# The search scores of the sample rows summed over heads in two passes of a split source, with the first projection tile of u placed among the last prompt scores

## What is computed

```python
def indexer_select(qi, wi, ki_all, q_pos, topk):
    s = jnp.einsum('bqhd,bld->bqhl', qi, ki_all) * (IDX_DIM ** -0.5)
    score = jnp.einsum('bqhl,bqh->bql', jax.nn.relu(s), wi) * (IDX_HEADS ** -0.5)
    score = jnp.where(admissible, score, NEG_INF)
    _, idx = lax.top_k(score, topk)
```

## Time and profile before

| | us |
|---|---|
| median of 3 runs | 1353.95 (1350.81 to 1354.22) |
| the profiled execution | 1354.13 |
| its span from first to last instruction | 1352.3 |
| PE busy | 1309.8 |
| DVE busy | 696.0 |
| POOL busy | 584.0 |
| ACT busy | 534.1 |

### The profile page before, as it was taken

How to read it: one execution, slowest core, us unless ns; L and a number is a source line. 1 busy time by engine, 2 the same in 40 slices (tenths; PEclk the granted TensorE clock), 3 DMA queues, 4 the chain that set the end, 5 groups by cost and what they waited for, 6 DMA issues and landing times.

```text
span 1352.3 us, 25244 instructions
## 1 busy us (share of the span) xinstructions
PE 1309.8 (97%) x9720; PEld 1212.9 (90%) x9720; DVE 696.0 (51%) x1611; ACT 534.1 (39%) x1075; POOL 584.0 (43%) x607
## 2 busy tenths in 40 slices
PE   5989999999999999999999999999999999999998
PEld 4957999995666899878999999999999999999997
DVE  5368997777985222227934434434544333333445
ACT  5345787747776322325533334334300110111034
POOL 5432975441331311321277667667433333333610
PEclk9999999999999999999999999999999999999999
DMA  6340113310001775782233323323531332133203
GB/s 195 74 104 17 46 42 112 94 50 1 1 12 37 265 231 192 237 281 95 80 112 126 111 81 127 111 80 127 192 112 47 111 112 93 66 112 111 63 1 128
DMA packets 143550, 141.68 MB, mean 105 GB/s; under 512 B 21081, under 2 KB 111321, under 8 KB 143424
## 3 DMA queue, kind: packets, MB, share of 16 engines
q1 hardware_dynamic: 124933, 116.31, 27.0%
q10 hardware_dynamic: 17842, 21.94, 4.5%
q0 software_dynamic: 656, 1.84, 0.6%
HBM read 111.87 MB, written 26.50 MB: 102 GB/s over the span
## 4 chain that ended last, share of the span: by engine, by line
PE 81%; DVE 6%; ACT 2%; issue 1%; POOL 0%; ACTq 0%; DVEq 0%; POOLq 0%
PE bank L2096 74%; PE bank L2272 2%; PE bank L2338 2%; DVE junk L1669 1%; ACT sjunk L1119 1%; PE bank L2417 1%; DVE prob L1762 1%; PE bank L2141 1%; DVE lack L1673 1%; PE bank L2605 0%; DVE hid_lo L2021 0%; DVE sqacc L1884 0%; DVE hn_lo L1897 0%; PE bank L2298 0%; DVE cum L1728 0%
## 5 line engine op out<-in xcount | busy, mean ns | idle before, releaser
L2096 PE MATMUL bank<-hid_hi,w_hi 128*128 128x384 f32 (+1 forms) x672 | 217.6, 324 | 0.0
L2096 PE MATMUL bank<-hid_lo,w_hi 128*128 128x384 f32 (+1 forms) x672 | 216.0, 324 | 0.8 <-DVE hid_lo L2021 0.8
L2096 PE MATMUL bank<-hid_hi,w_lo 128*128 128x384 f32 (+1 forms) x672 | 216.2, 322 | 0.0
L2053 DVE TENSOR_TENSOR acc<-bank,acc 128x384 f32<-128x384 f32 x168 | 87.6, 523 | 199.3 <-PE bank L2096 199.3
L690 POOL TENSOR_TENSOR w_hi<-w_raw,zero 128x256 fp32r<-128x256 f32 x108 | 68.7, 636 | 206.1 <-PE bank L2096 190.7
L2096 PE MATMUL bank<-xn_hi,w_hi 128*128 128x384 f32 (+1 forms) x456 | 151.3, 332 | 2.5 <-POOL w_lo L692 1.7
L904 POOL TENSOR_TENSOR w_hi<-w_raw,zero 128x1024 fp32r<-128x1024 f32 x29 | 54.9, 1894 | 221.3 <-PE bank L2096 203.3
L2096 PE MATMUL bank<-xn_lo,w_hi 128*128 128x384 f32 (+1 forms) x456 | 148.1, 325 | 0.0
L2096 PE MATMUL bank<-xn_hi,w_lo 128*128 128x384 f32 (+1 forms) x456 | 147.5, 323 | 0.0
L1416 ACT ACTIVATE hid_hi<-hraw 128x1056 fp32r<-128x1056 f32 x32 | 32.7, 1078 | 257.1 <-DMA hraw<-hidden_dram 130.2
L2096 PE MATMUL bank<-hi_T,hn_hi 128*128 128x264 f32 x448 | 127.5, 285 | 0.0
(11 more groups left out here) (300 smaller groups left out, 3212.0 us busy)
## 6 DMA issues: line engine op xcount, KB each, us to landing
w_raw<-in_w_ff_dram SPq DMA_DIRECT2D x50, 512.0 KB, 3.5
hraw<-hidden_dram SPq DMA_DIRECT2D x16, 1056.0 KB, 7.3
page<-in_cache_k_dram SPq DMA_DIRECT2D x64, 256.0 KB, 3.5
page<-in_cache_v_dram SPq DMA_DIRECT2D x64, 256.0 KB, 3.6
hidden_dram<-stg ACTq DMA_DIRECT2D x56, 264.0 KB, 2.0
w_raw<-in_w_in_dram SPq DMA_DIRECT2D x18, 512.0 KB, 3.7
wr<-in_w_ff_dram SPq DMA_DIRECT2D x14, 512.0 KB, 4.5
xrow<-in_x_prompt_dram SPq DMA_DIRECT2D x8, 512.0 KB, 8.2
```

The source lines that it names most:

```text
L2053: nc.vector.tensor_tensor(v, ps[:, 0:w], v, ALU.add).then_inc(freeof(("dn", gi, m, g)), 1)
L2096: return nc.tensor.matmul(out, lhsT, rhs, start=start, stop=stop)
```

## The change

The sum over heads is made from a split source. `hsum` is copied to `hsum_r` (rounded type, on ACT), `srel` is rounded into `srel_hi` on ACT and the rest goes to `srel_lo` on DVE, and each piece of the sum is two matmuls of the rounded type in place of one of float32. The pieces use banks 0, 1 and 2. The first tile of block 3 is computed ahead of the sum: its steps 0 to 2 (`US`) between the third and the fourth of the last score pieces, steps 3 to 7 behind the fourth.

```diff
@@ banks
         for i in range(3):
-            take(("ssum", i), 3 + i % 2)
+            take(("ssum", i), i)
@@ ACT
                     scores_relu(mixed(b))
+            for i, (c, w) in enumerate(S_COLS):
+                wait_evac(act, ("ssc", 2))
+                if i == 0:
+                    nc.scalar.activation(hsum_r[:, :], hsum[:, :], ACT.Copy).then_inc(s_hsr, 1)
+                nc.scalar.activation(srel_hi[:, c:c + w], srel[:, c:c + w], ACT.Copy).then_inc(s_srh, 1)
             scores_relu(mixed(NB))
@@ DVE
             sample_relu()
             scores_sum(mixed(NB))
+            for i, (c, w) in enumerate(S_COLS):
+                dve.wait_ge(s_srh, i + 1)
+                nc.vector.tensor_tensor(srel_lo[:, c:c + w], srel[:, c:c + w], srel_hi[:, c:c + w].bitcast(F),
+                                        ALU.subtract).then_inc(s_srl, 1)
@@ PE
-            prompt_scores(mixed(NB))
-            for i in range(3):
-                wait_evac(pe, ("ssc", i))
-            for i in range(3):
-                w = 512 if i < 2 else NS
+            prompt_scores(mixed(NB)[:3])
+            pe.wait_ge(s_wlo, N_U + 1)
+            proj_tile(N_U, 0, ks=range(US))
+            prompt_scores(mixed(NB)[3:])
+            proj_tile(N_U, 0, ks=range(US, KC))
+            pe.wait_ge(s_hsr, 1)
+            for i, (c, w) in enumerate(S_COLS):
                 ps = begin(pe, ("ssum", i))
-                mm(ps[0:NS, 0:w], hsum[:, :], srel[:, 512 * i:512 * i + w], True, True).then_inc(fullof(("ssum", i)), 1)
+                pe.wait_ge(s_srl, i + 1)
+                mm(ps[0:NS, 0:w], hsum_r[:, :], srel_hi[:, c:c + w], True, False)
+                mm(ps[0:NS, 0:w], hsum_r[:, :], srel_lo[:, c:c + w], False, True).then_inc(fullof(("ssum", i)), 1)
```

More of the change, by code:

```diff
@@ L132, in hymba_pool_dsa_step @@
         zqi = at("zqi", A_V + SK * 4, [P, 2, IH, NB * (NS + TS)], F)
+        srel_hi = at("srel_hi", A_V + SK * 4, [P, SK], R)
+        srel_lo = at("srel_lo", A_V + 2 * SK * 4, [P, SK], R)
+        hsum_r = at("hsum_r", A_V + 3 * SK * 4, [P, NS], R)
+        assert 2 * SK + NS <= 2 * IH * NB * (NS + TS)
         A_KT = A_V + (SK + 2 * IH * NB * (NS + TS)) * 4
@@ L433, in hymba_pool_dsa_step @@
         s_relu = sem("score_relu")
+        s_hsr, s_srh, s_srl = sem("head_sum_rounded"), sem("sample_scores_high"), sem("sample_scores_low")
         s_diag = sem("scores_causal")
@@ L526, in hymba_pool_dsa_step @@
         ROUNDS = 31
+        S_COLS = [(512 * i, 512 if i < 2 else NS) for i in range(3)]
         def rows_of(j):
@@ L2113, in three, with proj_tile @@
                 return mm(ps, a_lo, b_hi, False, end)
-            def proj_tile(n, g, by_k=False):
+            def proj_tile(n, g, by_k=False, ks=range(KC)):
                 wh = w_hi[n % 2][:, :].rearrange("p (k n) -> p k n", k=KC)
@@ L2118, in proj_tile @@
                 t0, w = TG[g]
-                ps = begin(pe, ("proj", n, g))
-                for k in range(KC):
+                ps = bank[plan[("proj", n, g)][0]] if ks[0] else begin(pe, ("proj", n, g))
+                for k in ks:
                     if by_k:
@@ L2124, in proj_tile @@
                                  k == 0, k == KC - 1)
-                last.then_inc(fullof(("proj", n, g)), 1)
+                if ks[-1] == KC - 1:
+                    last.then_inc(fullof(("proj", n, g)), 1)
             def proj(n, rows_src=None):
@@ L2129, in proj @@
                 for g in range(3):
-                    proj_tile(n, g)
+                    if (n, g) != (N_U, 0):
+                        proj_tile(n, g)
                     if rows_src is not None:
                         to_rows(n - 1, rows_src, g)
+            US = 3
             def to_rows(n, src, i):
```

## The result

The changed kernel takes 1358.0 us (median of 8 runs, 1356.23 to 1360.70), the kernel before, timed beside it, 1352.39 (8 runs, 1350.81 to 1354.22). The ratio is 1.0041, with a 95% interval of 1.0031 to 1.0051: 5.6 us slower. The profiled execution took 1358.04 us, with a span of 1356.2.

The account below looks back on a forecast made before the run. The search chain through DVE and ACT, not busy PE, was taken to decide when `utail` is copied. 1354.13 + 2.05 + 3.5 - 0.7 + 1.6 = 1360.6, as median 1360.4 us; own range 1358.5 to 1362.5, wide 1354.5 to 1363.5.

Parts of the forecast that it names:

- the wide one: Range of the whole time, 1354.5 to 1363.5 us, from the rival without collision and clock up to partial upper bounds.
- One sign that I had named for being wrong: Outside the handover and search: another stretch than 103 to 190 us changes by over 1 us.
- Search decides, PE's lead is worth nothing: At `utail`, 177.5 us: the search is later by 2.2 us, so PE's lead gains nothing and a later search costs its delay.
- the rival of the surviving lead: At 177.5 us PE's own tiles decide and PE keeps its 3.2 us: 1350.8 us, faster by 0.23%; chance 0.07.
- Term 1: Handover from scores to search: the search starts 2.05 us later, at 115.2 us for 113.14; bounds 1.6 and 2.8.
- the clock falls in the handover too: Behind PE's idle 1.7 us, fifteen matmuls run at half clock, the sum up to 1.5 us later: 1361.9 us; chance 0.12.
- Term 2: DVE's small steps and sign multiplications meet POOL's split of block 5: 3.5 us more; bounds 0.4 and 4.8.
- Term 3: First round of the search: two small steps are now free of the split of block 5, -0.7 us.
- The sum at `utail`: The copy of `utail` comes 2.05 + 3.5 - 0.7 = 4.85 us later, at about 182.4 us.
- The wait behind block 4: PE at the transposes behind block 4 waits 4.8 us for ACT's copies of block 3, off the deciding path.
- Term 4: Behind PE's wait at `utail` the clock falls to 0.50 and eleven matmuls lose 1.6 us; bounds 0 and 2.6.

Follow-up runs that it names:

- before, late: Kernel before with three more counts on DVE ahead of the search's first count, nothing else changed: 1358.64 us, ratio 1.0046.
- split only: Changed kernel with the first tile of u back behind the sum, the two-pass sum kept: 1356.04 us, ratio 1.0027.
- POOL waits: Changed kernel in which POOL holds the split of block 5 until DVE's sign multiplications are made: 1356.63 us, ratio 1.0027.
- changed free: Changed kernel with the transposes of block 7 in other banks, so bank 7 is needed one tile later: 1361.61 us, ratio 1.0057.
- tile only: Changed kernel with the old float32 sum behind the moved tile, without roundings and subtractions: 1356.18 us, ratio 1.0027.
- relus first: Changed kernel with only the last relu behind ACT's four roundings, the others ahead of them: 1355.81 us, ratio 1.0026.
- both: Changed kernel with only the last relu behind the roundings and POOL's split of block 5 behind the sign multiplications: 1353.61 us, ratio 1.0013.
- all three: Changed kernel with only the last relu behind the roundings, POOL's block 5 split behind the sign multiplications, and block 7's transposes in other banks: 1351.34 us, ratio 0.9999.
- before lead: Kernel before without 12 of 24 matmuls of u's first tile (u incomplete), POOL's block 5 split held until the sign multiplications are made: 1352.27 us, ratio 1.0000.
- before free lead: Kernel before with block 7's transposes in other banks, 12 matmuls of u's first tile left out and POOL's block 5 split held: 1352.26 us, ratio 1.0000.
- before, free: Kernel before with only the transposes of block 7 in other banks, so bank 7 is needed one tile later: 1350.17 us, ratio 0.9990.

## Why the prediction was right, and what in it was not

The forecast was 6.4 us above the kernel before, and the measured medians differ by 5.6. The forecast time of 1360.4 us is 2.4 above the measured 1358.0, of which 1.6 lie in the kernel before: the median of 3 runs that I started from was 1353.95, that of 8 is 1352.39. So 1358.0 is half a microsecond below the forecast's own range, 1358.5 to 1362.5, and inside the wide one. The direction and the mechanism hold; two of the four terms changed places.

One sign that I had named for being wrong did come, a change of over 1 us outside 103 to 190 us: `srel` ended 1.45 us earlier than before. It is no effect of the edit. The profile of the kernel before has a fall of the clock behind its early wait, and `srel` ends at 106.62 there and at 106.41 in "before, late", which has one as well; in the other twelve profiles it ends at 104.58 to 105.45.

- **Search decides, PE's lead is worth nothing.** Shown from both sides: a later search alone makes the kernel 6.0 us slower, a lead of 2.1 us alone gains 0.4 at most. The rival of the surviving lead falls with it.
- **Term 1, 2.05 us.** The steps came as written: ACT's roundings and the first late relu at 1.33 us behind `srel` (1.3 forecast), the sum on DVE at 1.94 (1.9). The search then started 3.70 us later and not 2.05, above the term's own bound of 2.8. The missing 1.65 is the rival "the clock falls in the handover too": ten of the fifteen matmuls behind the idle 1.84 us ran 0.32 apart, not 0.175, and the score piece ahead of them took 0.25 longer than forecast. I gave it 0.12. The clock fell there in all four profiled kernels whose relus stand behind the roundings (changed, split only, POOL waits, changed free), and in none of the four with a moved tile or relus first (tile only, relus first, both, all three). In the last four PE has no wait of over 0.4 us at that place. It belonged in the forecast.
- **Term 2, 3.5 us.** Measured 3.27 from the small steps to the first round. The price of one collision was right and the number of them was not. Of the seven multiplications five met the split and were 0.24 to 0.48 us longer, 5.82 - 3.81 = 2.0 together and 0.40 each for my 0.38; the last two ran behind it in their old time. I had counted all seven, 2.7. Three of the five small steps met it as well, 0.42 each, 1.3 in place of my 0.8. The clock in the handover did not undo the meeting, since PE and with it POOL came 1.65 us later too.
- **Term 3, -0.7 us.** From the first round to the release of the next, 4.64 us before and 3.90 after.
- **The sum at `utail`.** 3.70 + 3.27 - 0.7 is 6.2; `utail` came 5.70 later, so half a microsecond is gained among the later collisions, which I had taken as fixed: one small step (line 1673, 0.69 us at 172.00 before) took its free time of 0.18.
- **The wait behind block 4.** 4.8 us forecast, 4.56 measured. It is 4.56 in all four kernels with the moved tile and the collision, and 2.2 in the three with the moved tile in which POOL waits.
- **Term 4, 1.6 us at `utail`.** This step failed in the profiled execution: 2.45 us of waiting, where I had PE arrive 3.5 to 5 us early, and no fall. PE had lost more of its lead than the wait behind block 4, which I had counted: 1.7 us in the handover, and some 2.5 of the 4.92 us of matmuls at half clock behind block 4. This second loss costs nothing, for PE would have waited as much longer at `utail`. Why the clock stayed up behind the 2.45 us is open. With 1.65 in the handover in its place the sum came out nearly the same, which is luck in the bookkeeping and not in the mechanism. In other kernels with 2.5 to 3.0 us there, the clock fell in four (tile only, relus first, POOL waits, before late) and not in two (both, before lead).

## What to carry to other kernels

When an engine is busy all the time and yet has one wait on a slower chain, ask of an edit first whether it starts that chain earlier or later; PE time saved ahead of the wait was worth 0.4 of 2.1 us at most, and 3.7 us more on an engine busy for half of the span cost 6.0. Work that is added to an in-order queue belongs behind what others wait for: four copies of 1.3 us had the search start 3.6 us later than it did with the same copies behind three relus. And a lead moves the engines that follow it: look at what the earlier transfer, split or copy will run beside.

## What the runs showed of the hardware

- DVE's multiplications of float32 rows by a scalar and POOL's two-input operations hold each other up one by one: five multiplications of 0.55 to 0.76 us became 0.24 to 0.48 longer, and POOL's rose from 0.61 or 0.75 to about 1.0. The Trainium skill, "SBUF — State Buffer", in the part on its engine ports, describes an exclusive lock for the whole instruction between GpSimd and a VectorE operation in a two-port mode or with two inputs in SBUF: the one that starts first has it. The trace agrees. The three small steps of the changed kernel that are longer end within 0.03 us of the end of a split operation (122.09 and 122.06, 122.92 and 122.90, 126.62 and 126.59), and the one that began at 122.12, 0.02 us ahead of POOL's next, took its old 0.17. In the kernel before, a step of 0.17 us took 1.83 beside a long operation of POOL, and ended with it:

```profile
136.40 1.83 DVE L1673 TENSOR_TENSOR lack<-cnt,lim 128x7 f32<-128x7 f32 x1 [0.36 <-ACT sjunk L1119]
```

```profile
135.72 2.50 POOL L835 TENSOR_TENSOR pooled<-pwork,pooled 128x1056 f32<-128x1056 f32 x1
```

- Waits of PE of the same length and at the same place had a granted clock of 0.50 behind them in some profiles and not in others: the 1.40 us ahead of the float32 sum in three of six, the 2.2 us behind block 4 in one of three, and 2.9 to 3.0 us at `utail` in three of five. The 1.84 us ahead of the fourth piece (three profiles), the 3.4 of "split only" and the 4.56 behind block 4 (four profiles) had it each time, in the wait or behind it; 1.84 us at 74 us of the kernel before did not.
- The attention phase ran for 13.5 us at half clock in two of 14 profiles (changed free, before free lead) and at 1.00 in the others, although PE's waits there are the same few tenths. Such a stretch lowers the mean clock by 0.005. Executions of "before, free" and "changed, free" whose mean clock is lower by about that are some 5 to 6 us longer. That the other banks make them more frequent is suggested by the runs (four of 12 of "before, free" at 0.992, none of 75 of the kernel before below 0.995), but "before, lead", with the old banks, has one of 11 at 0.992. The cause stays open.
